# Weight-block sums of a seven-product up-projection: from GpSimd adds to accumulating DMAs, with weight splits two blocks at a time

## The reference, cut to what matters

```
def conv_ffn(h, w_in, conv_w, conv_b, w_out):
    u = h @ w_in                                   # 640 x 1024 by 1024 x 5632
    up = jnp.pad(u, ((0, 0), (1, 1), (0, 0)))
    uc = up[:, :-2] * conv_w[0] + up[:, 1:-1] * conv_w[1] + up[:, 2:] * conv_w[2] + conv_b
    a, b = jnp.split(uc, 2, axis=-1)
    return (jax.nn.silu(a) * b) @ w_out            # 2816 -> 1024
```

## Time and profile before

| | |
|---|---|
| median of 3 runs | 3258.68 us (3257.69 to 3265.19) |
| the profiled execution's own time | 3259.57 us, span 3257.8 us |
| TensorE busy in the span | 2968.5 us, 91% |
| VectorE busy | 2528.1 us, 78% |
| ScalarE busy | 1485.2 us, 46% |
| GpSimd busy | 1034.7 us, 32% |
| read from HBM | 283.98 MB, 88 GB/s over the span |

### The profile page before, as it was taken

One profiled execution on the slowest core, in us unless ns is written; L12 is line 12 of the kernel. 1 busy time (PEld: TensorE's weight loads), 2 busy tenths in 40 slices (PEclk: granted clock), 3 DMA queues, 4 the chain that ended last, 5 costly groups with the idle time before them and its releaser, 6 DMA issues. The chain is left out here.

```text
span 3257.8 us, 55789 instructions
## 1 busy us (share of the span) xinstructions
PE 2968.5 (91%) x19576; PEld 2666.9 (82%) x19576; DVE 2528.1 (78%) x4329; ACT 1485.2 (46%) x2996; POOL 1034.7 (32%) x808
## 2 busy tenths in 40 slices
PE   8799999999997999999999979999999899798889
PEld 6688888976697888898866778889898669698889
DVE  6888888778668788888657587887887766878887
ACT  3544444446544444444345353444453664444453
POOL 3422332133233223313257242232223223322331
PEclk9899999999998999999999999999999999899999
DMA  8433333210113333332100213333321011222211
GB/s 337 172 104 117 112 107 114 98 56 1 65 66 101 106 116 104 115 114 85 66 19 7 104 65 117 105 114 106 124 101 56 1 41 51 65 67 73 66 64 59
DMA packets 47207, 290.20 MB, mean 89 GB/s; under 512 B 4945, under 2 KB 11345, under 8 KB 13265
## 3 DMA queue, kind: packets, MB, share of 16 engines
q1 hardware_dynamic: 47058, 288.21, 26.2%
HBM read 283.98 MB, written 4.21 MB: 88 GB/s over the span
## 5 line engine op out<-in xcount | busy, mean ns | idle before, releaser
L2999 DVE SCALAR_TENSOR_TENSOR xT<-psB,mod,xT 128x128 f32<-128x128 f32 x750 | 378.3, 547 | 251.7 <-PE psB L2245 251.3
L2472 PE MATMUL psA<-h_hi,w_hi 128*128 128x320 f32 x1280 | 403.0, 315 | 30.8 <-DVE w_lo L3088 27.7
L2245 PE MATMUL psB<-g_hi,wo_hi 128*128 128x320 f32 x1280 | 319.2, 333 | 119.4 <-DVE xT L2999 119.4
L2206 POOL TENSOR_TENSOR w_stage<-w_stage,w_sum 128x512 f32<-128x512 f32 x76 | 98.8, 1300 | 955.2 <-DVE w_lo L3088 955.2
L2472 PE MATMUL psA<-h_lo,w_hi 128*128 128x320 f32 x1280 | 394.6, 309 | 5.8 <-issue 5.8
L2472 PE MATMUL psA<-t_lo,w_hi 128*128 128x320 f32 x1280 | 398.8, 312 | 0.0
L2472 PE MATMUL psA<-h_hi,w_lo 128*128 128x320 f32 x1280 | 395.3, 309 | 0.0
L3088 DVE TENSOR_TENSOR w_lo<-w_stage,w_hi 128x512 fp32r<-128x512 f32 x400 | 336.1, 850 | 48.7 <-ACT w_hi L2730 46.9
L2245 PEld LDWEIGHTS psB<-g_hi,wo_hi 128*128 128x128 f32 x1280 | 229.9, 204 | 141.5 <-DVE xT L2999 129.1
L2752 ACT ACTIVATE g_hi<-conv 128x128 fp32r<-128x128 f32 (+1 forms) x160 | 66.4, 462 | 542.1 <-PE psB L2245 516.0
L2245 PE MATMUL psB<-g_lo,wo_hi 128*128 128x320 f32 x1280 | 310.8, 326 | 0.0
(11 more groups left out here) (320 smaller groups left out, 7470.0 us busy)
## 6 DMA issues: line engine op xcount, KB each, us to landing
w_stage<-weights_dram SPq DMA_DIRECT2D x124, 1024.0 KB, 5.1
m_half<-w_mod_dram SPq DMA_DIRECT2D x62, 1024.0 KB, 5.1
wo_stage<-w_out_dram SPq DMA_DIRECT2D x44, 1024.0 KB, 4.8
m_stage<-w_mod_dram SPq DMA_DIRECT2D x24, 1024.0 KB, 8.8
m_gap<-w_mod_dram SPq DMA_DIRECT2D x10, 1024.0 KB, 7.8
yT_dram<-xT SPq DMA_DIRECT2D x8, 322.0 KB, 2.2
xT<-xT_dram SPq DMA_DIRECT2D x1, 1544.0 KB, 10.1
xT<-xT_dram SPq DMA_DIRECT2D x1, 1032.0 KB, 6.6
```

Of the source, the lines that this page charges most:

```text
L2206: pool.tensor_tensor(w_stage[:, 4 * p, :], w_stage[:, 4 * p + 1, :], w_part(it, p, 2), ALU.subtract).then_inc(s_ss, 1)
L2245: ins = pe.matmul(o, wp, xp[:, a:b], start=first and n == 0, stop=last and n == 2)
L2472: ins = pe.matmul(psA[:, bank, 0:HALF], w[:, q, c], x[q][:, k, :], start=(q in (0, 1, 3) and k == 0 and n == 0), stop=(k == 3 and n == 2), ...
L2999: ins = dve.scalar_tensor_tensor(out=xT[:, d, c:c + w], in0=tokens(ps, slot)[i], scalar=gate[:, d, i:i + 1], in1=xT[:, d, c:c + w], op0=AL ...
```

## The change

1. The weight blocks of a pair are loaded in four groups that already stand where the products want them: `GROUPS = ((0, 2), (2, 4), (4, 6), (6, 7))`, seven blocks (1.75 MiB) in place of four. Blocks 2 and 3, and 4 and 5, begin as copies of a11, a21 and of a11, a12.
2. GpSimd no longer adds. It starts four DMAs per pair that add to their destination (`accum_op=ALU.add`): two of 512 KiB from HBM, one of 256 KiB from HBM, one of 256 KiB from SBUF to SBUF. The last two each wait for one of the first two. The signs of two sums of `h`, of one split of `h` and of the taps of two of the four tiles are turned, so that only additions are needed.
3. ScalarE and VectorE split a group at a time: four instructions per pair (three of 1024 columns, one of 512) in place of seven of 512.
4. `last_half` moves from GpSimd to VectorE.
5. The orders of ScalarE and VectorE are rewritten, and SyncE waits per group and not per half.

The groups, and SyncE:

```diff
+        GROUPS = ((0, 2), (2, 4), (4, 6), (6, 7))
+        W_GROUPS = len(GROUPS)
...
+                def load_group(it, p, g):
+                    a, b = GROUPS[g]
+                    if isinstance(it, int) and (it, p) == (1, 0):
+                        sp.wait_ge(s_wlo, UNITS * oF + b)
+                    else:
+                        sp.wait_ge(s_slo, nth(l, it, p, W_GROUPS, g + 1 - W_GROUPS))
+                    u = 4 * p
+                    units = (slice(u, u + 2), slice(u, u + 4, 2), slice(u, u + 2), slice(u + 3, u + 4))[g]
+                    sp.dma_start(w_stage[:, a:b, :],
+                                 t["weights"][ds(it + cf, 1), :, :].rearrange("a p (u n) -> (a p) u n", n=UNIT)[:, units, :]
+                                 ).then_inc(s_pg[g], 16)
...
                 def ffn_loads(it):
-
-                    for half in range(2):
-                        sp.wait_ge(s_slo, nth(l, it, half, PRODUCTS, PRODUCTS))
-                        load_half(it + (cf + 1), half)
-                        if half == 0 and more:
-                            used_m_half(l, it, 0)
-                            load_m_half(l, it, 1)
+                    load_group(it, 1, 3)
+                    load_group(it + 1, 0, 0)
+                    load_group(it + 1, 0, 1)
+                    if more:
+                        used_m_half(l, it, 0)
+                        load_m_half(l, it, 1)
+                    load_group(it + 1, 0, 2)
                     if more:
                         used_m_half(l, it, 1)
                         load_m_half(l, it + 1, 0)
+                    load_group(it + 1, 0, 3)
+                    load_group(it + 1, 1, 0)
                     next_wo(it)
-
+                    load_group(it + 1, 1, 1)
+                    load_group(it + 1, 1, 2)
```

GpSimd, where the old `w_sums`, `w_last_sum`, `last_half` and the loop over them go:

```diff
+                    def begin(i, g):
+                        a, b = GROUPS[g]
+                        pool.wait_ge(s_pg[g], nth(l, it, p, 16, 16))
+                        pool.dma_start(w_stage[:, a:b, :],
+                                       t["weights"][it + cf:it + cf + 1, :, :]
+                                       .rearrange("a p (u n) -> (a p) u n", n=UNIT)[:, 4 * p + 2:4 * p + 4, :],
+                                       accum_op=ALU.add).then_inc(s_pa[i], 16)
+
+                    def end(i, out, src):
+                        pool.wait_ge(s_pa[i], nth(l, it, p, 16, 16))
+                        pool.dma_start(out, src, accum_op=ALU.add).then_inc(s_pb[i], 16)
+
+                    begin(0, 1)
+                    begin(1, 2)
+                    end(0, w_stage[:, 2, :], t["weights"][it + cf:it + cf + 1, :, (4 * p + 3) * UNIT:(4 * p + 4) * UNIT]
+                        .rearrange("a p n -> (a p) n"))
+                    end(1, w_stage[:, 5, :], w_stage[:, 4, :])
...
+                w_sums(1, 0)
                 pool.wait_ge(s_hf, KT * l + KT)
+                h_sum(0, f11, f11, f12, ALU.subtract)
+                h_sum(1, f12, f22, f12, ALU.subtract)
+                h_sum(2, f22, f22, f11, ALU.add)
+                h_sum(3, f21, f22, f21, ALU.subtract)
                 w_sums(1, 1)
+                for it in range(2, ITERS):
+                    for p in range(2):
+                        w_sums(it, p)
```

ScalarE's split, and its new order (only the added and kept lines):

```diff
+                def split_product(it, p, g):
+                    a, b = GROUPS[g]
...
+                        act.wait_ge(s_su, nth(l, it, p, PRODUCTS, b - PRODUCTS))
+                    act.wait_ge((s_pg[0], s_pb[0], s_pb[1], s_pg[3])[g], nth(l, it, p, 16, 16))
+                    act.activation(w_hi[:, a:b, :], w_stage[:, a:b, :], ACT.Copy).then_inc(s_shi, 1)
...
                     conv_first(it - 1, 3)
...
+                    split_product(it, 0, 3)
                     first_part(it, 0)
                     silu(it - 1, 1)
...
+                    second_part(it, 0)
                     split_product(it, 1, 0)
+                    ghi(it - 1, 1)
+                    third_part(it, 0)
+                    fourth_part(it, 0)
                     split_product(it, 1, 1)
                     conv_first(it, 0)
                     fifth_part(it, 0)
                     conv_first(it, 1)
+                    split_product(it, 1, 2)
 
                 def ffn_iter(it):
                     to_first_half(it)
+                    split_product(it, 1, 3)
                     silu(it, 0)
                     ghi(it, 0)
+                    first_part(it, 1)
                     wohi(it, 0)
                     split_product(it + 1, 0, 0)
                     wohi(it, 1)
                     second_part(it, 1)
+                    third_part(it, 1)
+                    split_product(it + 1, 0, 1)
+                    fourth_part(it, 1)
                     split_product(it + 1, 0, 2)
                     conv_first(it, 2)
```

VectorE's new order (again without the lines that go):

```diff
                     conv_end(it - 1, 3)
...
                     gate(it - 1, 1)
+                    product_lo(it, 0, 3)
                     add_first(it, 0)
...
+                    glo(it - 1, 1)
+                    product_lo(it, 1, 0)
+                    last_half(it, 0)
...
                     add_second(it, 0)
+                    product_lo(it, 1, 1)
                     conv_end(it, 0)
 
                 def ffn_iter(it):
                     to_first_half(it)
                     out_add(it - 1, 0)
+                    step = conv_left(it, 1, conv[1])
+                    out_add(it - 1, 1)
+                    conv_right(it, 1, conv[1], step)
+                    out_add(it - 1, 2)
                     gate(it, 0)
...
+                    out_add(it - 1, 4)
...
+                    out_add(it - 1, 5)
+                    product_lo(it, 1, 2)
+                    out_add(it - 1, 6)
+                    out_add(it - 1, 7)
...
+                    product_lo(it, 1, 3)
                     glo(it, 0)
                     wolo(it, 0)
                     product_lo(it + 1, 0, 0)
                     add_first(it, 1)
                     wolo(it, 1)
...
+                    product_lo(it + 1, 0, 1)
+                    last_half(it, 1)
                     add_second(it, 1)
+                    product_lo(it + 1, 0, 2)
```

More of the change, by code:

```diff
@@ L128, in __call__, with wait @@
         self.n += 1
-    def wait(self):
-        self.eng.wait_ge(self.sem, self.loop + self.n)
+    def wait(self, n=None):
+        self.eng.wait_ge(self.sem, self.loop + (self.n if n is None else n))
 def band_tiles(j):
@@ L197, in program @@
         g_lo_last = at("g_lo_last", [P, 2, TOK], F32R, B_T + 4 * KT * TOK + 8 * TOK)
-        w_sum = [at(f"w_sum{i}", [P, UNIT], F32, B_W + (1 + i) * W + 4 * (UNITS - 1) * UNIT) for i in range(2)]
         B_NORM = B_N + M + 8 * C
@@ L2092, in ffn_loads @@
                         load_m_half(l, it + 1, 0)
+                    load_group(it + 1, 0, 3)
+                    load_group(it + 1, 1, 0)
                     next_wo(it)
+                    load_group(it + 1, 1, 1)
+                    load_group(it + 1, 1, 2)
+                for g in range(W_GROUPS):
+                    load_group(1, 0, g)
+                if l == 0:
+                    sp.wait_ge(s_mraw, 2 * (MOD_PASSES - 1))
+                    load_m_half(0, 0, 0)
+                load_group(1, 1, 0)
+                next_wo(0)
+                if l == 0:
+                    used_m_half(0, 0, 0)
+                    load_m_half(0, 0, 1)
+                load_group(1, 1, 1)
+                load_group(1, 1, 2)
                 if more:
@@ L2548, in _, with split_w @@
             own = Steps(act, s_act)
-            def split_w(c, units, waits=None):
+            def split_w(n, units, waits=None):
                 for u in units:
@@ L2629, in _ @@
                             if c < nq - 1:
-                                split_w(c0 + c + 1, between.get(j, ()), waits=UNITS * (o0 + c))
+                                split_w(o0 + c + 1, between.get(j, ()), waits=UNITS * (o0 + c))
                             if l != 2 and (c, j) == (2, 2):
@@ L2856, in _ @@
                 for half in range(2):
[L2857 removed]
+                    act.wait_ge(s_o, KT * (ITERS * l + it) - KT // 2 * (1 - half))
                     c = slice(half * UNIT, (half + 1) * UNIT)
@@ L3044, in _ @@
                 norm_dve(2 * l + 1)
+                taps = vec[:, l * V_LAYER + V_CONV + 16:(l + 1) * V_LAYER].rearrange("p (i f c) -> p i f c", f=4, c=4)[:, :, 1:4:2, 0:3]
+                own(dve.tensor_scalar(taps, taps, -1.0, None, op0=ALU.mult))
                 for b in u_raw:
@@ L3084, in glo, with product_lo @@
                     ins.then_inc(s_g, 1)
-                def product_lo(it, p, q):
-                    dve.wait_ge(s_shi, nth(l, it, p, PRODUCTS, q + 1))
-                    dve.tensor_tensor(w_lo[:, q, :], w_part(it, p, q), w_hi[:, q, :].bitcast(F32),
+                def product_lo(it, p, g):
+                    a, b = GROUPS[g]
+                    dve.wait_ge(s_shi, nth(l, it, p, W_GROUPS, g + 1))
```

(9 more changed lines are left out.)

218 lines of the change are left out of this document (64 added, 154 removed).

## The result

The changed kernel takes 3449.4 us (median; 3435.3 to 3457.2), the kernel before 3261.9 beside it: 1.057 of its time, 95% interval 1.053 to 1.061. The forecast was 3074, its range ended at 3275. It is slower by 187 us, on the side of R4.

What follows compares the result with a forecast made beforehand. TensorE, 91% busy, was taken as the bound. Layers 0 to 2 give 108 us, layer 3 51, half clock minus 8, starts 28: 179; with 6 for punctual chains 185, from 3258.7 to 3074; range 3010 to 3275.

Steps and rivals of the forecast that it cites:

- R4: Rival, chance 0.17: accumulating DMA slower than three passes; TensorE stands twice a step, gain gone at x + y = 10.8; 3389 us.
- TensorE's floor: FFN step: products 24.6, output pass 14.1, two modulation halves of 1.0 each, transposes and hand-overs 1.0; sum 41.7 us.
- the contention: Before output tile 2: GpSimd's adds slow VectorE's convolutions, costing 2.45 us of TensorE's 2.99 us wait.
- R3: Rival, chance 0.09: GpSimd's building of DMA descriptors slows VectorE as its adds did; 3200 us.
- The 1.3 us a step for late sums: FFN step: 1.0 us lost to late accumulations, with GpSimd's DMA start estimated at 0.5 to 1, plus 0.3 for small waits.
- Chain B: Pair 0 of the next step: group 2's load, then second and third accumulations, before ScalarE's `fourth_part`; late by x + y - 7.8.
- Chain A: Pair 1 of the next step: group 2's load, then accumulations, before ScalarE's `conv_first`; late by x + y - 8.5.
- x + y: Times of one 512 KiB and one 256 KiB accumulating DMA, issue to landing; taken as 8.1 us, between 4.9 and 11.2.
- R2: Rival, chance 0.20: sums late by some us, x + y about 10, 3.7 us late per step; 3160 us.
- high end: Accumulating DMAs: source read, destination read and destination write one after another, making x + y 7.2 + 4.0 = 11.2 us.
- Layer start: First pair, before product 2: without weight sums on GpSimd, TensorE's 13.18 us wait shrinks; 7 us won per layer.
- At nothing: Parts counted as no gain or loss: negated taps (under 1 us in all), merged semaphores, moved modulation loads.

## Why the prediction was wrong

*TensorE's floor, the orders, the wide splits, the contention:* right. 41.7 us a step was forecast and 41.55 measured without sums, 0.88 for the convolution and 1.22 for the wide split stand in the trace. GpSimd's DMA instructions, 0.86 us each, don't slow VectorE: the convolution at 1197.57 runs beside one and takes 0.88. R3 falls.

*Place and order of the late sum:* right too. Both chains end with the third accumulation in GpSimd's order, which is group 1's last and stands behind group 2's first, and ScalarE holds `fourth_part` and `conv_first` for it, as R4 said. Two things were missing. In pair 1 "the first lies before" is false: the third starts 0.4 us after group 1's first has landed, so that chain is load, first and third on one buffer, 4.5 + 7.4 + 7.1 us and the 0.4; it is late even with group 2's sums left out. And group 2's own last sum, the fourth, has a deadline of its own in pair 0: 117.6 of ScalarE's 519.4 us.

*The 1.3 us a step for late sums: the step that failed.* The means of layers 0 to 2, from step 2 on, against the forecast (us; the first measured line is from the run without sums, the rest from the changed kernel; late is the sum of the three lines above it against the forecast's deadlines, 37.8 and 53.5):

| | Chain B forecast | measured | Chain A forecast | measured |
|---|---|---|---|---|
| group 2 free | 26.1 | 26.4 | 41.8 | 42.3 |
| to the second accumulation's start | 3.9 | 4.1 | 3.2 | 5.3 |
| from there to the third's landing (x + y) | 8.1 | 10.1 | 8.1 | 9.8 |
| late | 0.3 | 2.8 | none | 3.9 |
| TensorE's wait there | | 2.2 | | 3.9 |

So x + y, put at 8.1, measured 10.1 and 9.8, and chain A's load took 2.1 more. The two waits, 1.3 us more for `part_y`, and the half clock behind them (a granted clock of 0.93 over these steps, for 1.00 without sums, some 3.7 us a step) add up to 11.1; the step is 52.6 - 41.6 = 11.0 longer than without sums. I had counted 1.3, and for the half clock behind late sums nothing, though rows 3 show it behind the old wait.

*What made x + y larger.* My rule for the second read (two passes, the write hidden) holds for the rate: 173 GB/s against 345 as copies. But even the copies of GpSimd take 4.9 us for 512 KB and 4.4 to 5.0 for 256 KB, against my plain 3.0 and 1.9. In that run SyncE's own loads of 512 and 256 KB land in 3.9 and 4.6, so half of the excess for 512 KB and nearly all of it for 256 is not GpSimd's: the line through the earlier trace rows was too low with other DMAs under way. GpSimd's part shows at the start: the first packet of its copies comes 1.5 us after the instruction starts, SyncE's after 0.96 (medians, where no other DMA of that engine is under way). The Trainium skill, *DMA: Bandwidth & Descriptors*, *Anatomy of one DMA — SWDGE (gpsimd) path*, gives 2.0 us plus bytes over 436 GB/s, an estimate of 3.2 and 2.6 us for the two sizes; the copies of this case, with others in the queue, took 4.9 and 4.4 to 5.0. The measurement decides.

*The rivals.* R2's condition came true, x + y about 10, and R4's result. R4 named the mechanism: ScalarE holding `fourth_part` and `conv_first`, TensorE standing twice a step. But its turning point of 10.8 was not reached. Its formula gives 10.1 + 9.8 - 16.3 = 3.6 us late; 6.7 were measured by the same deadlines, since group 2 is free and loaded later than forecast, and 11.0 lost, since it has neither the fourth accumulation nor the half clock. I had given R4 0.17 and ended the range at 3275, though the forecast's own high end stood past the turning point and no row bounded the adding rate. That was the error of judgement: the two ends' middle is no evidence.

*Layer start:* 7 us each were forecast. In layers 1 to 3 of the run without sums step 1 is 12.4, 11.4 and 13.9 us shorter than before, a later step 5.6, 5.5 and 7.5, so the start gives 6 to 7: right. With the sums the wait before product 2 is 8.5 us for 13.2, but step 1 of these layers is only 1.1, 3.7 and 1.4 us shorter. *"At nothing":* the moved modulation load showed a wait of 12.7 us, and taking it away won nothing. *The gain* was nearly right: I counted 226 us with all chains on time, and 241 lie between the kernel before and the one without sums; the new orders alone are worth 96 of them.

What isn't settled: why the changed kernel's late sums come out as an irregular step (48.6 to 57.1 us in layer 0), what GpSimd does in the 1.6 us behind the landed load, and how the lateness divides between queue and chain.

## What to carry to other kernels

When work leaves a busy engine for the DMA queues, price the turnaround of the buffer, not the engines' share: load, sum and sum again ran one after the other, 6.7, 5.8 and 5.1 us in the step of the last run with a second buffer, and between the buffer's release and ScalarE's wish for it lay 11.9. The DMA engines were 74% to 84% busy in such steps, so waiting in the queue is a part of those times. If contention between two engines hurts at one place, first try to move the work in time: one wait added to GpSimd won 73 us, at no cost in bytes. And where a price has no row, let the range reach past the turning point of the rival that hangs on it.

## What the runs showed of the hardware

- An accumulating DMA kept the DMA engines busy twice as long per byte as a copy of the same bytes: 173 against 345 GB/s.
- GpSimd spent 0.86 us on most of the DMAs it started (1.06 on average on the third of each pair), and a VectorE instruction beside one stayed at 0.88 us.
- After the wait of 2.92 us at 1245.85 the granted clock was 0.50, TensorE's level of 1.2 GHz and not 2.4, for about 3 us, and its matmuls started 0.27 us apart in place of 0.147; after 2.18 us, in the run with new orders, the granted clock of the step stayed 1.00:

```profile
1246.00:1249.00 3.00, 3.00 (x12) 3.00 (x13) 1.46 (x3) 0.59 (x1) 0.00 (x0) 0.50 0.79 165
```

- Beside each other VectorE and GpSimd slow down by different shares: VectorE's convolution takes 1.85 us for 0.88 (x2.1), GpSimd's add 1.62 to 1.87 for the 1.29 of the run with held sums (x1.3 to 1.5).
- GpSimd's adds beside VectorE cost a kernel 223 us by what they slowed, though GpSimd was busy only 32% of the time. With the new orders and the adds held behind addition 2 the kernel is 74 us above the one without sums (3093.2 against 3019.6), which has the wide splits besides.
